# State space channel's gate made at the end of the second mixer's projections, its scaling and split inside the output product

## The reference, cut to what matters

```python
h = modulate(rms_norm(x), sh_m, sc_m)
proj = h @ w_in[l]
z = proj[..., :D_SHIFT]            # 1792 columns, for the RWKV channel
u = proj[..., D_SHIFT:]            # 512 columns, for S5
...
y = (einsum(c_re, s_re) - einsum(c_im, s_im) + d_skip * ug).reshape(bsz, seq, D_S5)
zz = jax.nn.gelu(y)
out = zz * jax.nn.sigmoid(zz @ w_glu + b_glu)          # w_glu is 512 x 512
return (rms_norm(out) * gain).astype(out_dtype)
...
mix = jnp.concatenate([y_rwkv, y_s5], axis=-1) @ w_out[l]   # 1024 x 1024
x = x + g_m[:, None, :] * mix
```

## Time and profile before

| | us |
|---|---|
| median of 3 runs | 3888.74 |
| the profiled execution | 3891.31 |
| its span (first to last instruction) | 3889.5 |
| `projections2_and_s5`, from the first product to the start of the next phase | 2234.3 to 2494.4 |
| `rwkv` | 2494.4 to 2915.9 |
| `s5_gate` | 2915.9 to 3003.0 |
| `residual_gemm` "mix2_out", products | 3003.1 to 3091.7 |

### The profile page before, as it was taken

The page is one execution under the profiler, slowest core; times in us unless marked ns, Lnnn a source line. Parts: engine busy times, 40 slices in busy tenths (PEclk is TensorE's granted clock), DMA queues, the critical chain, the costliest instruction groups (busy, mean ns, idle before and its releaser), DMA issues. The chain is left out here.

```text
span 3889.5 us, 55742 instructions
## 1 busy us (share of the span) xinstructions
PE 3510.9 (90%) x23201; PEld 2896.4 (74%) x23201; DVE 1777.2 (46%) x2725; ACT 868.9 (22%) x1258; POOL 1032.2 (27%) x491
## 2 busy tenths in 40 slices
PE   5999999988989889999999789688874889999997
PEld 4878777767777777888888678577763778888886
DVE  4752555324777635555555535144433322323233
ACT  2012122122334212111111220244322131111112
POOL 3333333333110333212212144132202332222121
PEclk7999999999999999999999899889886999999998
DMA  3353433342000312322222164200002111111111
GB/s 97 130 177 115 124 102 109 103 123 81 8 5 1 128 44 76 119 87 73 88 70 81 44 168 120 82 19 34 5 3 94 51 50 40 58 38 59 38 49 44
DMA packets 309559, 285.55 MB, mean 73 GB/s; under 512 B 21326, under 2 KB 276864, under 8 KB 308408
## 3 DMA queue, kind: packets, MB, share of 16 engines
q1 hardware_dynamic: 283882, 209.82, 18.3%
q10 hardware_dynamic: 25186, 72.62, 5.0%
q0 software_dynamic: 288, 0.20, 0.0%
HBM read 221.64 MB, written 60.95 MB: 73 GB/s over the span
## 5 line engine op out<-in xcount | busy, mean ns | idle before, releaser
L710 POOL TENSOR_TENSOR ffn_wlo<-ffn_raw,ffn_whi 128x1024 fp32r<-128x1024 f32 x88 | 211.4, 2404 | 1067.7 <-ACT ffn_whi L898 1011.8
L203 PE MATMUL up<-h_hi,ffn_whi 128*128 128x512 f32 x1408 | 439.0, 393 | 22.0 <-POOL h_lo L404 22.0
L203 PE MATMUL up<-h_lo,ffn_whi 128*128 128x512 f32 x1408 | 435.5, 391 | 0.0
L203 PE MATMUL up<-h_hi,ffn_wlo 128*128 128x512 f32 x1408 | 434.8, 390 | 0.0
L192 POOL TENSOR_TENSOR whi<-raw,ones 128x1024 fp32r<-128x1024 f32 (+1 forms) x87 | 159.2, 1830 | 800.3 <-PE acc L1406 452.0
L203 PEld LDWEIGHTS up<-h_hi,ffn_whi 128*128 128x128 f32 x1408 | 263.1, 189 | 80.1 <-POOL h_lo L404 15.6
L203 PEld LDWEIGHTS up<-h_lo,ffn_whi 128*128 128x128 f32 x1408 | 265.3, 188 | 56.1
L203 PEld LDWEIGHTS up<-h_hi,ffn_wlo 128*128 128x128 f32 x1408 | 265.1, 188 | 55.9
L1406 PE MATMUL acc<-h_hi,whi 128*128 128x512 f32 x816 | 270.7, 413 | 8.7 <-POOL h_lo L404 8.7
L801 DVE TENSOR_TENSOR ffn_prod<-ffn_act,up 128x1024 f32<-128x1024 f32 x44 | 53.7, 1222 | 464.5 <-PE up L203 459.8
L1406 PE MATMUL acc<-h_lo,whi 128*128 128x512 f32 x816 | 255.4, 395 | 0.0
(11 more groups left out here) (543 smaller groups left out, 6618.5 us busy)
## 6 DMA issues: line engine op xcount, KB each, us to landing
raw<-w_in SPq DMA_DIRECT2D x51, 512.0 KB
projT<-proj_stage ACTq DMA_DIRECT2D x51, 512.0 KB, 2.7
ffn_ada_raw<-w_ada SPq DMA_DIRECT2D x24, 1024.0 KB, 5.0
ffn_raw<-w_up SPq DMA_DIRECT2D x44, 512.0 KB
ffn_draw<-w_down SPq DMA_DIRECT2D x11, 1024.0 KB, 6.7
ffn_raw<-ffn_w_gate SPq DMA_DIRECT2D x22, 512.0 KB
ffn_raw<-ffn_w_up SPq DMA_DIRECT2D x22, 512.0 KB
ffn_draw<-ffn_w_down SPq DMA_DIRECT2D x11, 1024.0 KB, 4.8
```

Of the source, the lines that this page charges most:

```text
L203: last = nc.tensor.matmul(acc[:, t, :], w[:, k, w_cols], x[:, k, t * HALF:(t + 1) * HALF], start=(k == 0 and i == 0), stop=(k == k_tiles - ...
L710: nc.gpsimd.tensor_tensor(w_lo[i][:], raw[i][:], w_hi[i][:], ALU.subtract).then_inc(s[f"up_split{i}"], 1)
```

## The change

The gate moves into the projection phase as four more slots, 17 to 20, ahead of the last `z` unit, which becomes slot 21. `Y_SLOT` goes from 14 to 13. Its inputs are loaded back by SP at slots 15 to 18, turned into `zz`, `z_hi`, `z_lo` by ACT (`channel`) and DVE (`low_part`) at slots 15 and 16. Each gate unit has 4 k tiles; its epilogue also adds up the squares, and ACT stores the gated tile to DRAM (`gated`). The sum over channels is made in slot 21 after k tile 5 (`gate_total`, 8 matmuls with one column), the reciprocal and root are taken on 128x8, and `gate_spread` (a transpose and 8 matmuls) spreads it over partitions; ACT copies it out and stores it to DRAM (`gate_rs`). `s5_gate` is gone. The `GatedTiles` object in "mix2_out" loads `gate_rs`, `gated` and the two halves of `xT` on ACT's queue (0.5, 2, 2 and 2 MB), scales and splits tiles 4 to 7 and lets PE wait for them from k tile 4 on. Nothing of `w_out` is prefetched any more (`first=None`).

```diff
-    Z_SLOT, SCAN_SLOT, Y_SLOT = 7, 9, 14
+    N, NU, NG = N_PROJ2 + 4, N_PROJ2 - UU, 4
+    Z_SLOT, SCAN_SLOT, Y_SLOT, GLU_SLOT = 7, 9, 13, N_PROJ2 - 1
+    units[GLU_SLOT:GLU_SLOT] = [None] * NG
...
 SP, in the loop over slots
+                view = w_glu(u - GLU_SLOT) if is_gate(u) else w_in2[:, :, t * P:(t + 1) * P]
+                sp.dma_start(raw[b][:, 0:tiles_of(u), :], view).then_inc(s[f"weight_loaded{b}"], 16)
+                if Y_SLOT + 2 <= u < Y_SLOT + 2 + NG:
+                    h = u - Y_SLOT - 2
+                    if h == 0:
+                        sp.wait_ge(s["states_done"], 2)
+                    for o in range(2):
+                        sp.wait_ge(s[f"y_stored{(2 * h + o) % 4}"], 16 * STEP * (h // 2 + 1))
+                    sp.dma_start(yin[h][:], yperm[h * P:(h + 1) * P]).then_inc(s[f"y_in{h}"], 16)
...
-                if u == 15:
+                if u == Y_SLOT + 1:
                     sp.wait_ge(s["toep_zero"], 1)
...
 PE
+                if u == GLU_SLOT:
+                    pe.wait_ge(s["z_split"], NG)
+                x_hi, x_lo = (z_hi, z_lo) if is_gate(u) else (hi, lo)
...
+                    if u == N - 1 and k == 5:
+                        gate_total()
+                    if u == N - 1 and k == n - 1:
+                        gate_spread()
...
 ACT
+            def channel(h):
+                if h == 0:
+                    act.wait_ge(s["y_done"], 8)
+                act.wait_ge(s[f"y_in{h}"], 16)
+                nc.scalar.activation(zz[:, h, :]..., yin[h][:]..., ACT.Gelu_apprx_tanh).then_inc(s["gelu_done"], 1)
+                act.wait_ge(s["gelu_done"], h + 1)
+                nc.scalar.activation(z_hi[:, h, :], zz[:, h, :], ACT.Copy).then_inc(s["z_high"], 1)
...
             for u in range(N):
                 if u > 0:
+                    gate(u - 1) if is_gate(u - 1) else store(u - 1)
+                if Y_SLOT + 2 <= u < Y_SLOT + 4:
+                    channel(2 * (u - Y_SLOT - 2))
+                    channel(2 * (u - Y_SLOT - 2) + 1)
...
+            act.wait_ge(s["gate_inverse"], 2)
+            nc.scalar.activation(compact[:], compact[:], ACT.Sqrt).then_inc(s["gate_root"], 1)
             store(N - 1)
+            act.wait_ge(s["gate_turned"], 1)
+            nc.scalar.activation(row[:], ps["tot"][0:NT, 1, 0:P], ACT.Copy).then_inc(s["gate_row"], 1)
+            act.wait_ge(s["gate_spread"], 1)
+            nc.scalar.activation(rs[:], ps["tot"][:]..., ACT.Copy).then_inc(s["rs_copied"], 1)
+            act.wait_ge(s["rs_copied"], 1)
+            act.dma_start(gate_rs, rs[:]).then_inc(s["rs_stored"], 16)
+            act.wait_ge(s["rs_stored"], 16)
...
 GatedTiles, in the phase of mix2_out
+        @block.scalar
+        def _(act):
+            act.dma_start(rs[:], self.gate_rs).then_inc(s["rs_in"], 16)
+            act.dma_start(zz[:], self.gated).then_inc(s["gated_in"], 16)
+            for i in range(2):
+                act.dma_start(xT[:, 4 * i:4 * i + 4, :], self.xsave[:, 4 * i:4 * i + 4, :]).then_inc(s[f"x_back{i}"], 16)
+            for k in range(4):
+                act.wait_ge(s["gated_scaled"], k + 1)
+                nc.scalar.activation(hi[:, 4 + k, :], zz[:, k, :], ACT.Copy).then_inc(s["hi_done"], 1)
+        @block.vector
+        def _(dve):
+            dve.wait_ge(s["rs_in"], 16)
+            dve.wait_ge(s["gated_in"], 16)
+            for k in range(4):
+                nc.vector.scalar_tensor_tensor(out=zz[:, k, :], in0=zz[:, k, :], scalar=prm[:, c:c + 1], in1=rs[:], ...)
+                dve.wait_ge(s["hi_done"], k + 1)
+                nc.vector.tensor_tensor(lo[:, 4 + k, :], zz[:, k, :], hi[:, 4 + k, :], ALU.subtract).then_inc(s["lo_done"], 1)
+    def ready(self, pe, k):
+        if k >= 4:
+            pe.wait_ge(self.s["lo_done"], k - 3)
...
-    s5_gate(nc, mem, env, yperm, xsave, ins, h)
-    residual_gemm(nc, mem, env, "mix2_out", columns(ins["w_out_2"], KD), h, KD, 0, sums, gate=ADA + 16)
+    residual_gemm(nc, mem, env, "mix2_out", columns(ins["w_out_2"], KD), h, KD, None, sums, gate=ADA + 16,
+                  norm=GatedTiles(nc, mem, env, gated, gate_rs, xsave))
```

More of the change, by code:

```diff
@@ L540, in _, with residual_gemm @@
                 sp.wait_ge(s[f"row_stored{b}"], 16 * (NT // 2))
-def residual_gemm(nc, mem, env, name, weight, rhs, k_tiles, first, sums, gate=None):
+def residual_gemm(nc, mem, env, name, weight, rhs, k_tiles, first, sums, gate=None, norm=None):
     xT, prm = env["xT"], env["prm"]
@@ L3370, in chunk_outputs, with gate_total, gate_spread @@
                 last.then_inc(s["y_done"], 1)
+            tot = ps["tot"]
+            def gate_total():
+                pe.wait_ge(s["gate_summed"], NG)
+                for i in range(NT):
+                    last = nc.tensor.matmul(tot[:, 0, i:i + 1], gsums[:, i * P:(i + 1) * P], env["ones"][:, 0:1], start=True, stop=True)
+                last.then_inc(s["gate_total"], 1)
+            def gate_spread():
+                pe.wait_ge(s["gate_root"], 1)
+                nc.tensor.transpose(tot[0:NT, 1, 0:P], compact[:], env["ident"][:]).then_inc(s["gate_turned"], 1)
+                pe.wait_ge(s["gate_row"], 1)
+                for i in range(NT):
+                    h, c = divmod(i * P, HALF)
+                    last = nc.tensor.matmul(tot[:, h, c:c + P], env["ident"][0:NT, i:i + 1].broadcast_to([NT, P]), row[:], start=True, stop=True)
+                last.then_inc(s["gate_spread"], 1)
             for u in range(N):
-                b = u % 2
+                b, n = u % 2, tiles_of(u)
                 pe.wait_ge(s[f"weight_split{b}"], u // 2 + 1)
@@ L3510, in _, with __init__, programs @@
                     states(u - SCAN_SLOT - 1)
+            dve.wait_ge(s["gate_total"], 1)
+            nc.vector.tensor_scalar(compact[:], ps["tot"][:, 0, 0:NT], 1.0 / HALF, EPS, ALU.mult, ALU.add).then_inc(s["gate_inverse"], 1)
+            dve.wait_ge(s["gate_inverse"], 1)
+            nc.vector.reciprocal(compact[:], compact[:]).then_inc(s["gate_inverse"], 1)
             read(N - 1)
[L3514 to L3530, removed]
+class GatedTiles:
+    SEMS = "gated_in rs_in x_back0 x_back1 gated_scaled "
+    pool_unit = 1
+    def __init__(self, nc, mem, env, gated, gate_rs, xsave):
+        self.nc, self.env, self.gated, self.gate_rs, self.xsave = nc, env, gated, gate_rs, xsave
+        self.zz = mem.at("mix2_gated", 136, [P, 4, S])
+        self.rs = mem.at("mix2_rs", 152, [P, S])
+    def programs(self, block, s, tot, at):
+        nc, prm, hi, lo, zz, rs, xT = self.nc, self.env["prm"], self.env["hi"], self.env["lo"], self.zz, self.rs, self.env["xT"]
+        self.s = s
@@ L3704, in build @@
     xsave = scratch("xsave", [P, KD, S])
+    gated = scratch("gated", [P, 4, S])
+    gate_rs = scratch("gate_rs", [P, S])
     s5d = dict(vin=scratch("s5_vin", [P, GP, 2, P]), wc=scratch("s5_wc", [P, 2, GP, STEP + 1, S5_C]),
```

140 lines of the change are left out of this document (61 added, 79 removed).

## The result

The changed kernel takes 3865.61 us (median of 4 runs, 3863.18 to 3868.61), beside 3887.26 for the kernel before in the same session; the ratio is 0.9938, with a 95% interval of 0.9924 to 0.9952. That is 21.7 us less; 19.2 less were forecast. The profiled execution took 3864.79 us.

The account below looks back on a forecast made before the run. It took PE to bound the projections and a chain of waits, no engine, the stretch behind the recurrence. 3891.31 + 40.2 - 59.4, less 2.6 for the median, gave 3869.5 us; own range 3862 to 3877, 8 in 10 within 3852 to 3882.

Parts of the forecast that it names:

- the projection phase: Phase that takes in the gate, bound by PE: its added costs sum to +40.2 us, from 34 to 49.
- behind R: From R, the recurrence's end, to the output product's first matmul: 87.2 us shrink to 27.8, saving 59.4.
- rival A: Output product: first weights land early, about R + 5, `gated` ends unit 0; 73.0 us saved, 3855.9 us; chance 0.20.
- Gate units: Four added gate slots in the projection phase, 5.44 us each at full clock, nothing hiding them: 21.8 us.
- The band: Slot 13: PE waits for the band's loads after GpSimd clears it; 4.8 us, from 3 to 5.2.
- The gate's inputs: Ahead of the first gate unit: PE waits for the inputs' readout, `channel`s and low part; 3.4 us.
- The clock: PE restarting at half clock after the waits at the band and the gate: 2.5 us for both, 0 to 5.4.
- The last split: Slot 21's full-size weights, split during slot 20 beside a busy DVE: 1.0 us, from 0 to 2.5.
- The total: Sum over channels in slot 21 after k tile 5: 1.8 us at full clock, 3.54 at half.
- The tail: From the last product to the next phase's start, with the gate row spread and stored: 11.3 us, 4.9 more.
- the arrival of the first weights: Output product: `w_out`'s first unit shares DMA one for one with ACT's loads, so first matmul at R + 27.8.
- Rival C: PE's clock, down in the wait at the first gate unit, stays down through slot 21: 3901 us; chance 0.05.

Follow-up runs that it names:

- e1: The changed kernel with 24 added matmuls, their result overwritten, keeping PE busy ahead of the band's wait in slot 13; 3861.08 us, ratio 0.9914.
- e2: The changed kernel with 24 overwritten matmuls ahead of the band's wait and 16 ahead of the first gate unit; 3857.63 us, ratio 0.9905.
- e6: The changed kernel with `gated` in four loads, `xT` loaded by SP behind the second weights, GpSimd's second split after the fourth low part; 3861.20 us.
- e5: The changed kernel with SP loading the output product's first weights only once `gate_rs` has landed; 3866.06 us, ratio 0.9939.
- e9: The changed kernel, but `gate_rs` and `gated` loaded, scaled and split in their own phase behind the recurrence; 3888.39 us, ratio 0.9994.
- e4: The changed kernel with `gated` loaded in four tiles and ACT waiting for the second unit's weights before loading `xT`; 3856.79 us, ratio 0.9906.
- e7: The kernel before with only the gate's scaling and splitting moved into "mix2_out", the gate staying behind the recurrence; 3884.82 us, ratio 0.9990.

## Why the prediction came out right, and where it was wrong

The forecast was 3869.5, the result 3865.61, inside the forecast's own range of 3862 to 3877. The sign held, and so did the shape: some 40 us more in the projection phase, more than that saved behind R. That the number came so close was luck. The projection phase cost 6.0 us more than put, and what lies behind R saved 9.6 more than put, because the wait that I put last there was not the last. What happened behind R is rival A, which had 0.20.

*The projection phase*: +46.2 (+43.6 in the second profile) against +40.2.

- Gate units, 5.44 us apart: right, 21.8.
- The band: 4.8 put, 5.5 and 4.1 measured. Right, within the bounds given (3 to 5.2), but for 0.3.
- The gate's inputs: 3.4 put, 3.8 measured in both profiles.
- **"The clock", put at 2.5 for both restarts with 5.4 as the most, is the term that was mis-sized.** Taken away by e1 and e2 it shows 6.3 us at the band (6.5 of stage, of which 0.2 is the wait's own length) and 1.7 at the gate: 8.0. Against the repeat it is some 5 at the band (3.9 of stage, and PE's start behind slot 12's read-out is 1.2 later in e1). I took the price from the output product's start, where matmuls of 512 columns ran back to back behind the wait and the fourth pair, 2.7 us later, was already fast. In the other profiles such matmuls stayed at half clock for up to 6.1 us (e6), so one row was too few. Behind the band come 128-column products in short groups, and the share stayed at 0.50 for 12.7 us (10.6 in the repeat). That the kind of matmul makes the stretch long is my guess: no run changes what follows the wait, and the last 5.3 us of the 12.7 were 512-column products too.
- The last split: 1.0 put, 0.2 measured; beside a busy DVE it took 5.5 us, as in the earlier trace rows, but slot 20's 5.44 covered all but that.
- The total: 1.8 put, 2.2 measured (13.25 - 10.88 - 0.2).
- The tail: 11.3 put, 11.1 measured.
- The range of the sum, "from 34 to 49", is a little narrow below: the terms' own lower bounds add up to 32.6. It doesn't matter here.

*Behind R*: -69.0 to the first addition (99.7 before, 30.7 after), -68.7 to the third, against -59.4.

- The step that failed is the arrival of the first weights: "R + 21.5" and the first matmul at "R + 27.8". They were there at R + 5.3. The rule behind it, one piece for one, is right: e5 shows it with 16.6 us for a unit and PE's start at R + 26.0, e9 with 13.8. What I had not counted is what SP's queue does in the time before ACT's large pieces come: nearly all of a unit's 1024 pieces, at up to 582 a us. I had written that against myself in rival A and given it 0.20. The two small terms around it, 0.9 us before the first piece and 1.0 behind the last, had no row behind them; q1's first pieces moved in the half us from R + 0.7. It is not a settled order: the seven profiles in which SP issues the weights as ACT issues `gate_rs` have them at R + 5.3 (three times), 5.6, 5.7, 8.8 and 13.2. The last is the repeat of the changed kernel, with R at 2955.87:

```profile
2969.07 1.89 POOL L192 TENSOR_TENSOR whi<-raw,ones 128x1024 fp32r<-128x1024 f32 x1 [14.24 <-DMA raw<-w_out]
```

There 1280 of q1's pieces had moved before the large ones ran, more than a unit has, so some of the first unit's must have been passed by those of the second on other engines; the queue's rows don't tell which, and this stays open. The head start makes an early landing likely, then, and doesn't assure it. Nor does a late one cost its whole delay: with the weights at R + 5.3, 13.2 and 20.1 (e5) the third addition came at R + 52.8, 55.1 and 61.4.
- Rival A had the mechanism, the early weights and DVE's chain as what ends unit 0, but 73.0 saved against 69.0 measured: `gated` came 0.8 us later (10.8 for 10.0), the last scaling and low part beside GpSimd's split took 2.6 us more where 1.0 was allowed, and the last k tile ran at half clock, 1.4 more. With the 6.0 of the projection phase that makes its 3855.9 some 10 too low, further off than the forecast whose last wait was wrong.
- My criterion "the prediction is wrong if the first weights aren't the last thing that unit 0 waits for" is met, so for this half it was wrong: right in sign and within 10 us, by the wrong last wait.

*Rival C*, the clock staying down over the gate's units, did not happen: the share from 2507 to 2522 is 1.00. Its mechanism did, at the band, for 12.7 us.

*What each half of the change is worth.* By stages, each half from one profile, against the mean of the two profiles of before: the move alone -1.8, merging alone -7.0, both -23.2. The parts don't add. The move alone leaves a chain of its own behind R, loads, four scalings, barrier, then weights in the open; the merging alone finds nothing else to hide under. Together the loads, the scalings and the weights' load lie beside each other, and that, -23.2 + 1.8 = -21.4 us, is nearly the whole gain of the changed kernel. Part of it is the queues' order: e9's weights took 13.8 us to land where the changed kernel's took 5.3. I had not told the two apart in the prediction.

## What to carry to other kernels

A wait on PE costs what stands in its bracket plus the clock behind it, and that price varies from place to place and from run to run (1.4 to 6.3 us here): look up the pair times of just the matmuls behind it, and where the wait can't go, fill it with matmuls whose result is overwritten (here 24 of them won 3.9 to 6.5 us, in a phase that PE bounds). When a load is uncovered, ask which queue starts first and what stands ahead on the other, not only how they share: with a small transfer ahead of the large ones SP's weights landed by R + 5.7 in five of seven profiles, and without it (e9) after 13.8 us. And before a two-part change is written off or praised for one part, build each alone: here neither is worth a fifth of a per cent, and both are worth 0.6%.

## What the runs showed of the hardware

- DVE operations with two SBUF operands are held up beside GpSimd's elementwise splits, not slowed evenly: 1.28 us becomes 2.92 (after), 3.29 and 3.42 (e4), 3.41 (e7), and the low part's 1.23 becomes 2.17, while GpSimd's second half goes from 2.34 to 3.21. Each of these DVE operations ends 1.07 to 1.09 us after the GpSimd operation that ran when it started, whatever was left of that: by the rows above 2982.59 and 2983.68, 2985.88 and 2986.97 in the profile after, 3001.22 and 3002.29 in e7. Spreading loads so that DVE starts earlier moved the scalings onto the split and won 1.2 us of the 3.1 offered. The Trainium skill has this in "Trainium Architecture — The Big Picture", What this means for kernel authors: the port that the two engines share is locked by one at a time, its bandwidth not split. The traces agree: one operation waits out the other (the 1.07 to 1.09 us above), and the prediction, which allowed 1.0 for it in rival A, should have priced a whole operation.
- Two DMA queues shared the engines piece for piece with pieces of 16 KB beside ones of 512 bytes (143 to 144), so 512 KB in 512-byte pieces took 13.8 us (e9) or 16.6 us (e5) beside large ones, and 5.3 us in three profiles (up to 13.2 in the others) when the large ones started a little later. With the 4 KB pieces of `gate_rs` the counts were not always even (32 to 261 in one us); the rows don't show single engines.
- After 4.45 us without work the clock share was at 0.50 again (2987 to 2990), and one k tile took 2.7 us rather than 1.36. The later window of the profile after:

```profile
2987.00:2990.00 3.00, 2.99 (x7) 2.43 (x8) 0.02 (x1) 0.00 (x0) 0.00 (x0) 0.50 0.58 174
```

- The fall can come behind the wait. In the repeat of the changed kernel PE waited 4.1 us for the band and restarted at 2412.31 at full clock. From 2413.3 on it ran at half, four matmuls taking 1.22 us where four such had just taken 0.71, until 2423.9, 10.6 us in all. In the first profile the share from 2412 to 2414 was 0.88, so it fell at 2413.5, half a us ahead of PE's restart. Both falls lie 5.0 to 5.1 us after PE's last matmul ahead of the wait, whether PE had restarted or not. The rows of the repeat:

```profile
2412.70 0.71 PE L3396 MATMUL zy<-s_sT,s_wc 64*128 64x128 f32 x4
...
2414.01 1.22 PE L3396 MATMUL zy<-s_sT,s_wc 64*128 64x128 f32 x4
```
